# Turning the FFN input of blocks 1 to 5 to channels: 120 TensorE transposes, or VectorE 32x32 blocks and transfers between partitions

## The chip, the cores and the metric

The kernel runs on one NeuronCore of a Trainium2 chip. The metric is the device time of one execution in microseconds, as the median of several runs. Times inside an execution come from a profile of one execution.

## The reference, cut to what matters

One layer of an encoder, over 128 sample tokens (8 sequences of 16) and 2048 prompt tokens, width 1024, all float32:

```python
h = rmsnorm(x, g_pre_mix) * (1 + sc1) + sh1          # adaLN; sc, sh, gt from silu(c) @ w_ada
proj = h @ w_in                                       # 1024 -> 2176
ya, yb, yc = pool_mixer(proj), conformer_conv(proj), short_conv(proj)
x = x + gt1 * rmsnorm(concat(ya, yb, yc) @ w_out, g_post_mix)
h = rmsnorm(x, g_pre_ffn) * (1 + sc2) + sh2           # "FFN input" below
f = (silu(h @ w_gate) * (h @ w_up)) @ w_down          # 1024 -> 2816 -> 1024
x = x + gt2 * rmsnorm(f, g_post_ffn)
```

## The kernel before, in words

The 17 tiles of 128 tokens are worked in six blocks: block 0 has two tiles, blocks 1 to 5 three each (`NT`). Every weight is streamed from HBM for every block in units of 128 x 1024 floats (512 KB). A unit is split into a high and a low float32r part: ScalarE writes `whi` (`high`, L980), VectorE `wlo` (`low`, L1377), and TensorE does three float32r matmuls in place of one in float32. Units are named by what they are for: `in` (17 per block, ORDER), `out` (8), `gu` (gate and up, 44) and `dn` (down, 22). For a block c of 1 to 4 the order of units (STREAM) is: out of block c, in of block c+1, dn of block c-1, gu of block c. Block 5 has no `in` units after its `out`.

Nothing is scheduled at run time. Each engine has its own instruction list, written out by hand, and runs it strictly in order; semaphores tie the lists together. Three distances matter here:

- SyncE issues the transfer of unit n when TensorE is done with unit n-6 (`RING` = 6, `load`, L476), that is, as TensorE begins unit n-5.
- ScalarE and VectorE split unit n+4 at the place of unit n in their lists (`LEAD` = 4, `ahead`). At the place of `in` unit j ScalarE's list has `ahead("in", c+1, j)` first, so the split of the unit four further on, and behind it `evacuate(c+1, j)`, which copies the finished projection out of PSUM (L1068, L1075). At the place of `dn` unit k it has the split of unit k+4 and behind it `hidden_high(c-1, k+2)`, the high part of the hidden activations for `dn` unit k+2 (L1141); VectorE has the low part (L1429) in the same way.
- TensorE's `project(c+1, j)` waits until `evacuate(c+1, j-2)` has freed its PSUM bank, and `down(c-1, k)` for the high and low hidden activations of k.

The FFN input of block c is made this way. ScalarE normalises the three token tiles from `xr` into `xt` (L1013), token-major: 128 tokens on the partitions, 1024 channels along the free axis. TensorE needs channels on the partitions. So during the `dn` units of block c-1, after unit 6, 8, ... 20, TensorE turns one chunk of 128 channels of three tiles: three transposes (L720) against the identity into a PSUM bank. ScalarE adds scale and shift while it copies out (`modulate`, L1048, into `h_f`) and writes the high part (`h_split`, L1059); VectorE writes the low part (`h_rest`, L1422). 8 chunks x 3 tiles x 5 blocks are 120 transposes. Block 0 does the same at another place and isn't changed. The projection input of blocks 2 to 5 (`by_channel`) is loaded from HBM with channels first and has no transposes.

Of the kernel before, what the change touches and what calls it, by code (L numbers as in the profile page):

```python
# [17 lines left out]
TB = 3  # L18
# [160 lines left out]


def transposed(q):

    return sum(not by_channel(i) for i in range(q))

# [43 lines left out]
def build(nc, x_all, x_cols, c_all, consts, consts_a, cols, gpost, b_ada, w_ada, w_mix, w_pool, w_gu, w_dn,  # L228
# [3 lines left out]
    with ctx:  # L232
# [31 lines left out]
        xt = sb("xt", [P, TB, D])  # L264
        xr = sb("xr", [P, TB, D])
        junk = sb("junk", [P, D], BF16)
        ssq_x = sb("ssq_x", [P, TB])
# [70 lines left out]
        xn_ready = sem("xn_ready")  # L338
        t_full = sem("t_full")
        t_read = sem("t_read")  # L340
        sample_mod = sem("sample_mod")
# [74 lines left out]
        def sum_bank(r, t):  # L416

            return 0 if r == RES.index(("mix", NB - 1)) and t == 0 else 2 + 2 * t

        def bank_pair(bank):  # L420
            return ps[:, bank:bank + 2, :].rearrange("p a n -> p (a n)")
# [16 lines left out]
        def h_float(q, k):  # L438
            if NORMS[q][1] == 0:
                return (h_wait if q else h_first)[:, k, :]  # L440
            if by_channel(q):
                return x_chunk(k)
            return h_f[:, k % 2, :]
# [15 lines left out]
        def _(sp):  # L459
# [85 lines left out]
            load_four(7)  # L545

            def store_gate(i):
                sp.wait_ge(gates_made, i + 1)
                sp.dma_start(gates[i], (gate1, gate2)[i][0:ROWS, :]).then_inc(gates_stored, 16)
# [21 lines left out]
            for c in range(NB):  # L571
# [9 lines left out]
                if c + 1 < NB:  # L581
                    for j in range(0 if c else EARLY, NIN):
                        load("in", c + 1, j)
                        if c == 0 and j == EARLY:
                            load_gate(0)
                        if c == 0 and j == NIN - 3:
                            store_gate(1)
                        if c == 0 and j == NIN - 1:
                            load_gate(1)
                        if c == 0 and j == EARLY + 2:  # L590
                            store_states(False)
                        if j == 12:
                            store(x1_v, "mix", c)
                        if j == 15 and c:
                            wait_stored("mix", c)
                            sp.wait_ge(xn_ready, transposed(norm("F", c) + 1))
                            load_res(x1_v, c - 1)
                if c:
                    for k in range(NF):
                        load("dn", c - 1, k)  # L600
                        if c == NB - 1 and k == 11:
                            store(x1_v, "mix", c)
                        if c == NB - 1 and k == 14:
                            wait_stored("mix", c)
                            sp.wait_ge(xn_ready, transposed(norm("F", c) + 1))
                            load_res(x1_v, c - 1)
                for m in range(NF):
                    for i in range(2):
                        load("gu", c, m, i)
                    if m == 4 and c + 2 < NB:  # L610
                        sp.wait_ge(t_full, KD * transposed(norm("F", c) + 1))
                        if c:
                            sp.wait_ge(res_tiles, res_all(RES.index(("ffn", c - 1))))
                        sp.dma_start(xt[:, :, :].rearrange("p t d -> p (t d)"), x_cols[c]).then_inc(cols_landed, 16)
                    if m == 7 and c:
                        store(y_v, "ffn", c - 1)
                    if m == 9:
                        if c:
                            wait_stored("ffn", c - 1)
                        else:  # L620
                            wait_stored("mix", 0)
                            sp.wait_ge(xn_ready, transposed(norm("F", 0) + 1))
# [25 lines left out]
        def _(pe):  # L648
# [62 lines left out]
            def transposes(q, k):  # L711
                if k == 0:
                    pe.wait_ge(xn_ready, transposed(q + 1))
                if q == norm("F", 0) and k < 2:
# [116 lines left out]
            def gate_up(b, m):  # L831
                q, w = norm("F", b), NT[b] * P
                for i in range(2):
# [3 lines left out]
                    elif m == 0 and b == 0:  # L837
                        pe.wait_ge(evac_done, evac_count(1, NIN - 2))
                    elif m == 0:
                        pe.wait_ge(t_read, KD * q + KD - 1 + i)  # L840
                    elif i == 0:
# [94 lines left out]
            for c in range(NB):  # L936
# [37 lines left out]
        def _(act):  # L974
# [56 lines left out]
            def modulate(q, k):  # L1031
# [20 lines left out]
            def h_split(q, k):  # L1052
# [4 lines left out]
                if q == norm("F", 0):  # L1057
                    act.wait_ge(*((h_free, k + 1) if k < KD - 1 else (w_used, UNIT["in", 1, NIN - 1] + 1)))
                nc.scalar.activation(h_hi[:, k, 0:w], h_float(q, k)[:, 0:w], ACT.Copy).then_inc(h_hi_ready, 1)  # L1059

# [157 lines left out]
            for c in range(NB):  # L1218
# [29 lines left out]
                if c:  # L1248
                    if c + 1 == NB:
                        mix_squares("mix", c)  # L1250
                    for k in range(NF):
# [9 lines left out]
                        ch = (k - 6) // 2  # L1261
                        if k >= 6 and k % 2 == 0 and ch < KD:
                            modulate(norm("F", c), ch)
# [97 lines left out]
        def _(dve):  # L1361
# [49 lines left out]
            def scale(q, k):  # L1411
# [19 lines left out]
            def weigh(kind, b, i):  # L1431
# [3 lines left out]
                if i == 0:  # L1435
# [3 lines left out]
                    else:  # L1439
                        dve.wait_ge(t_full, KD * transposed(norm("F", c) + 1 if c < NB else len(NORMS)))  # L1440
                dve.wait_ge(mix_ssq, tiles_before_res(r) + i + 1)
# [314 lines left out]
            for c in range(NB):  # L1756
# [35 lines left out]
                if c:  # L1792
# [3 lines left out]
                    for k in range(NF):  # L1796
# [3 lines left out]
                        if c + 1 == NB and k < NT[c]:  # L1800
                            join("mix", c, k)
                        ch = (k - 6) // 2
                        if k >= 6 and k % 2 == 0 and ch < KD:
                            h_rest(norm("F", c), ch)
# [127 lines left out]
```

## Time and profile before

| | us |
|---|---|
| median of 3 runs (lowest, highest) | 2260.72 (2260.14, 2261.42) |
| span of the profiled execution, first to last instruction | 2256.9 |
| TensorE busy in it | 2241.4 |
| VectorE busy | 1348.1 |
| ScalarE busy | 1003.7 |
| GpSimd busy | 38.2 |
| share of the 16 DMA engines used by queue 1 | 47.8% |

The profiled execution is reported by its span, 2256.9 us; a whole execution has besides that what lies before the first and after the last instruction. The median of the runs is 3.8 us above the span. TensorE's granted clock is 0.999 of full speed. Durations of matmuls in the trace overlap: the hardware pipelines them, so the distance between two starts is the time that one takes of the engine. "SPq" rows are SyncE's issues of transfers: the time is that of the issuing, which holds back the next instruction of SyncE, not that of the transfer.

### The profile page before, as it was taken

What the parts mean: (1) busy time and instruction counts of PE and PEld (TensorE: products, weight loads), DVE (VectorE), ACT (ScalarE), POOL (GpSimd) and SP (SyncE); (2) the same over time, 40 slices, a digit from 0 to 9 for tenths busy, and PEclk for the clock granted to TensorE, in tenths of its full rate; (3) what the DMA queues carried; (4) which work ended last, traced back from release to release, by engine and by line L of the source; (5) the groups of instructions that cost most, each with busy time, mean ns of one, the idle gap of its engine ahead of it and who ended that gap; (6) DMA issues with size and microseconds to landing.
All of it is one profiled execution on the core that took longest, in us unless ns stands there. A gap on an engine that the chain in (4) does not pass through costs nothing.

```text
span 2256.9 us, 29984 instructions
## 1 busy us (share of the span) xinstructions
PE 2241.4 (99%) x12270; PEld 2069.5 (92%) x12270; DVE 1348.1 (60%) x1967; ACT 1003.7 (44%) x1419; POOL 38.2 (2%) x83
## 2 busy tenths in 40 slices
PE   9999999999999999999999999999999999999998
PEld 6779998979999988999898899989899998899987
DVE  3779966698444677744467854357784535443343
ACT  3455465454354534344544435254443425432332
POOL 0000000000000000000000000000000000000000
PEclk9999999999999999999999999999999999999999
DMA  9864654554443533544353363435335444444332
GB/s 375 310 218 168 239 202 140 177 169 166 170 151 129 181 127 122 186 150 154 126 185 123 123 213 122 157 123 187 122 127 181 123 131 154 154 150 159 123 129 94
DMA packets 103046, 368.98 MB, mean 163 GB/s; under 512 B 12631, under 2 KB 14807, under 8 KB 102396
## 3 DMA queue, kind: packets, MB, share of 16 engines
q1 hardware_dynamic: 102910, 367.06, 47.8%
q8 instruction: 98, 1.61, 0.3%
q14 instruction: 38, 0.31, 0.0%
HBM read 348.02 MB, written 19.00 MB: 163 GB/s over the span
## 4 chain that ended last, share of the span: by engine, by line
PE 89%; DVE 4%; DMA 1%; ACT 1%; issue 0%; SPq 0%; DVEq 0%; ACTq 0%
PE ps L650 89%; DVE wlo L1377 2%; DVE pr L1528 1%; DMA raw<-in_w_mix 1%; PE ps L720 1%; DVE early L1528 1%; PE ps L680 0%; DVE g_lo L1429 0%; ACT whi L980 0%; DVE h_lo L1422 0%; DMA raw<-in_w_gu 0%; ACT h_f L1048 0%; DVE xt L1446 0%; ACT junk L1003 0%; DVE pr L1550 0%
## 5 line engine op out<-in xcount | busy, mean ns | idle before, releaser
L1377 DVE TENSOR_TENSOR wlo<-raw,whi 128x1024 fp32r<-128x1024 f32 x531 | 646.6, 1222 | 521.9 <-ACT whi L980 520.6
L650 PE MATMUL ps<-h_hi,whi 128*128 128x384 f32 (+1 forms) x2808 | 920.9, 328 | 1.8 <-DVE h_lo L1422 1.0
L980 ACT ACTIVATE whi<-raw 128x1024 fp32r<-128x1024 f32 x531 | 560.8, 1058 | 811.6 <-DMA raw<-in_w_gu 528.7
L650 PE MATMUL ps<-h_hi,wlo 128*128 128x384 f32 (+1 forms) x2808 | 919.3, 327 | 0.0
L650 PE MATMUL ps<-h_lo,whi 128*128 128x384 f32 (+1 forms) x2808 | 919.2, 327 | 0.0
L650 PEld LDWEIGHTS ps<-h_hi,whi 128*128 128x128 f32 x2808 | 528.4, 188 | 7.0 <-issue 4.7
L650 PEld LDWEIGHTS ps<-h_lo,whi 128*128 128x128 f32 x2808 | 528.4, 188 | 0.5
L650 PEld LDWEIGHTS ps<-h_hi,wlo 128*128 128x128 f32 x2808 | 528.4, 188 | 0.0
L650 PE MATMUL ps<-whi,g_hi 128*128 128x512 f32 x748 | 235.1, 395 | 1.7 <-issue 0.9
L650 PE MATMUL ps<-whi,g_lo 128*128 128x512 f32 x748 | 231.1, 390 | 0.0
L650 PE MATMUL ps<-wlo,g_hi 128*128 128x512 f32 x748 | 230.8, 390 | 0.0
L1528 DVE SCALAR_TENSOR_TENSOR pr<-u,col,pr 128x384 f32<-128x384 f32 x360 | 208.3, 613 | 1.0
L1837 DVE TENSOR_TENSOR g_f<-ps,s_buf 128x384 f32<-128x384 f32 (+1 forms) x132 | 70.3, 533 | 218.3 <-PE ps L650 218.1
L650 PEld LDWEIGHTS ps<-wlo,g_hi 128*128 128x128 f32 x748 | 140.4, 188 | 29.9
L650 PEld LDWEIGHTS ps<-whi,g_lo 128*128 128x128 f32 x748 | 140.4, 188 | 29.7
L650 PEld LDWEIGHTS ps<-whi,g_hi 128*128 128x128 f32 x748 | 136.8, 188 | 31.1 <-DVE g_lo L1429 4.1
L650 PE MATMUL ps<-whi,y_pr 128*128 128x512 f32 x476 | 131.1, 389 | 0.0
L1068 ACT ACTIVATE pr<-ps 128x384 f32<-128x384 f32 (+1 forms) x84 | 39.3, 470 | 153.5 <-PE ps L650 153.4
L650 PEld LDWEIGHTS ps<-whi,y_pr 128*128 128x128 f32 x476 | 89.2, 188 | 18.3
L1048 ACT ACTIVATE h_f<-ps,shsc 128x384 f32<-128x384 f32 x48 | 32.2, 670 | 140.4 <-PE ps L720 125.5
L1422 DVE TENSOR_TENSOR h_lo<-h_f,h_hi 128x384 fp32r<-128x384 f32 x48 | 26.7, 557 | 83.7 <-ACT h_hi L1059 83.7
L1429 DVE TENSOR_TENSOR g_lo<-g_f,g_hi 128x384 fp32r<-128x384 f32 (+1 forms) x132 | 69.9, 529 | 11.4 <-ACT g_hi L1141 11.4
(148 smaller groups left out, 1313.6 us busy)
## 6 DMA issues: line engine op xcount, KB each, us to landing
raw<-in_w_gu SPq DMA_DIRECT2D x264, 512.0 KB, 3.3
raw<-in_w_mix SPq DMA_DIRECT2D x150, 512.0 KB, 3.3
raw<-in_w_dn SPq DMA_DIRECT2D x132, 512.0 KB, 3.3
xr<-in_x_all SPq DMA_DIRECT2D x29, 512.0 KB, 5.9
xr<-x_all SPq DMA_DIRECT2D x17, 512.0 KB, 5.8
pre<-in_w_ada SPq DMA_DIRECT2D x16, 512.0 KB, 10.4
x_all<-xr SPq DMA_DIRECT2D x5, 1536.0 KB, 7.5
xr<-in_w_ada SPq DMA_DIRECT2D x12, 512.0 KB, 7.9
```

Source lines behind the costliest of these rows:

```text
L650: return nc.tensor.matmul(out, lhsT, rhs, start=start, stop=stop, skip_group_check=True)
L720: last = nc.tensor.transpose(ps[:, t_bank(q, k), t * P:(t + 1) * P], xt[:, t, k * P:(k + 1) * P], ident)
L980: nc.scalar.activation(whi[:, s, :], raw[:, s, :], ACT.Copy).then_inc(w_hi, 1)
L1048: nc.scalar.activation(h_float(q, k)[:, c0:w], src, ACT.Identity, scale=shsc[:, 2 * ph + 1, k, 0:1], bias=shsc[:, 2 * ph, k, 0:1])\
L1068: i = nc.scalar.activation(dst, src, ACT.Sigmoid if kind == "g" else ACT.Copy)
L1377: tt(wlo[:, s, :], raw[:, s, :], whi[:, s, :].bitcast(F32), ALU.subtract).then_inc(w_lo, 1)
L1422: tt(h_lo[:, k, 0:w], h_float(q, k)[:, 0:w], h_hi[:, k, 0:w].bitcast(F32), ALU.subtract)\
L1429: tt(g_lo[:, s, 0:w], g_f[:, k, 0:w], g_hi[:, s, 0:w].bitcast(F32), ALU.subtract).then_inc(g_lo_ready, 1)
L1528: i = stt(z, conv_in(j, k), wk, src, ALU.mult, ALU.add)
L1837: tt(g_f[:, m, 0:w], ps[:, gu_bank(m, 1), 0:w], s_buf[:, m % 2, 0:w], ALU.mult).then_inc(g_ready, 1)
```

## The change

For blocks 1 to 5 (`turned`), the 120 transposes leave TensorE's list. VectorE turns each normalised token tile in 32x32 blocks, from `xt` into a new buffer `turn` (`turn_tile`, one instruction of 128 x 1024 floats a tile, 15 in all). That leaves every 32x32 block turned within its own strip of 32 partitions. SyncE then moves strip a's blocks to the strips where their channels belong (`turn_back`): for each tile 4 x 4 transfers, each of 32 partitions x 8 chunks x 32 floats, so 256 runs of 128 bytes and 32 KB; 48 transfers a block, 240 in all. They write into `xt`, now with channels on the partitions, and ScalarE's `modulate` works in place there and no longer reads PSUM or writes `h_f`. The waits that stood on the transposes move to other semaphores; in block 5 the eight chunks are made at `dn` units 13 to 20, one each, in place of every second one of 6 to 20. The scratch memory for GpSimd's transfers, of which there are none, is cut to 1024 bytes, which makes room for `turn`.

```diff
+def turned(q):
+    return NORMS[q][0] == "F" and NORMS[q][1] >= 1
+def f_chunks(c, k):
+    at = k - 13 if c == NB - 1 else (k - 6) // 2 if k % 2 == 0 else -1
+    return [at] if 0 <= at < KD else []
...
+            def turn_back(b):
+                q = norm("F", b)
+                sp.wait_ge(turn_full, turned_tiles(q + 1))
+                for t in range(NT[b]):
+                    for a in range(STRIPS):
+                        for s in range(STRIPS):
+                            src = strips(turn[:, t, :], a).rearrange("p (k m) -> p k m", k=KD)[:, :, C_PAD * s:C_PAD * (s + 1)]
+                            n0 = t * P + C_PAD * a
+                            dst = strips(xt[:, :, :].rearrange("p t d -> p (t d)").rearrange("p (k n) -> p k n", k=KD), s)
+                            sp.dma_start(dst[:, :, n0:n0 + C_PAD], src).then_inc(turn_landed, 16)
...
                             load_res(x1_v, c - 1)
+                        if j == 16 and c:
+                            turn_back(c)
...
                         if c == NB - 1 and k == 14:
                             wait_stored("mix", c)
...
                             load_res(x1_v, c - 1)
+                            turn_back(c)
...
                         down(c - 1, [k])
-                        ch = (k - 6) // 2
-                        if k >= 6 and k % 2 == 0 and ch < KD:
-                            if ch == 0 and c + 1 < NB:
-                                pe.wait_ge(evac_done, evac_count(c + 1, NIN - 1))
-                            transposes(norm("F", c), ch)
...
+                elif turned(q):
+                    act.wait_ge(turn_landed, 16 * STRIPS * STRIPS * turned_tiles(q + 1))
+                    src = x_chunk(k)[:, c0:w]
...
+            def turn_tile(b, t):
+                q = norm("F", b)
+                dve.wait_ge(xn_ready, normalised(q + 1))
+                if t == 0:
+                    dve.wait_ge(turn_landed, 16 * STRIPS * STRIPS * turned_tiles(q))
+                nc.vector.transpose(turn[:, t, :], xt[:, t, :]).then_inc(turn_full, 1)
...
+                        if c and j0 + 7 <= j < j0 + 7 + NT[c]:
+                            turn_tile(c, j - j0 - 7)
...
+                        if c + 1 == NB and k == 5:
+                            for t in range(NT[c]):
+                                turn_tile(c, t)
```

SyncE's list around the step from the `in` units of block 3 to the `dn` units of block 1, before (w_mix is `in` and `out`, the store and `xr` loads are residuals):

```order
L488 DMA x_all<-xr 128x3x1024
L476 DMA raw<-in_w_mix 128x1024 x3
L484 DMA xr<-x_all 128x1024 x3
L476 DMA raw<-in_w_mix 128x1024
L476 DMA raw<-in_w_dn 128x1024 x22
```

and the same place now:

```order
L515 DMA x_all<-xr 128x3x1024
L503 DMA raw<-in_w_mix 128x1024 x3
L511 DMA xr<-x_all 128x1024 x3
L503 DMA raw<-in_w_mix 128x1024
L583 DMA xt<-turn 32x8x32 x48
L503 DMA raw<-in_w_dn 128x1024 x22
```

The 48 transfers of the block stand between the last `in` unit's load and the first `dn` unit's.

ScalarE's list at the last `in` units of block 3, the same before and now but for line numbers (whi is the split of the unit four ahead; pr and xa are evacuations of the unit itself, here units 12 to 16; g_hi is hidden activations):

```order
L980 ACTIVATE whi<-raw 128x1024
L1068 ACTIVATE pr<-ps 128x384
L980 ACTIVATE whi<-raw 128x1024
L1068 ACTIVATE pr<-ps 128x384
L980 ACTIVATE whi<-raw 128x1024
L1068 ACTIVATE pr<-ps 128x384
L980 ACTIVATE whi<-raw 128x1024
L1075 ACTIVATE xa<-ps 128x384
L1141 ACTIVATE g_hi<-g_f 128x384
L980 ACTIVATE whi<-raw 128x1024
L1075 ACTIVATE xa<-ps 128x384
L1141 ACTIVATE g_hi<-g_f 128x384
```

The second whi here is that of `dn` unit 0, and the evacuation of `in` unit 13 stands behind it. Nothing moved.

VectorE's list at the `in` units 7 to 9 of block 3, now (u and pr are steps of the depthwise convolution):

```order
L1423 TENSOR_TENSOR wlo<-raw,whi 128x1024
L1470 STREAM_TRANSPOSE turn<-xt 128x1024
L1581 SCALAR_TENSOR_TENSOR pr<-u,col,pr 128x384 x3
L1423 TENSOR_TENSOR wlo<-raw,whi 128x1024
L1470 STREAM_TRANSPOSE turn<-xt 128x1024
L1555 TENSOR_TENSOR u<-pr 128x384
L1581 SCALAR_TENSOR_TENSOR pr<-u,col,pr 128x384
L1578 TENSOR_SCALAR pr<-u,col 128x384
L1423 TENSOR_TENSOR wlo<-raw,whi 128x1024
L1470 STREAM_TRANSPOSE turn<-xt 128x1024
```

Before, the same rows stood there without the three STREAM_TRANSPOSE.

## Rows read from the trace of the kernel before

**Rows 1.** The page: its head and part 1 (busy us, share, instructions).
```profile
span 2256.9 us, 29984 instructions
PE 2241.4 (99%) x12270; PEld 2069.5 (92%) x12270; DVE 1348.1 (60%) x1967; ACT 1003.7 (44%) x1419; POOL 38.2 (2%) x83
```
**Rows 2.** Waits, whole span: who waited for whom, us in total, times, longest.
```profile
ACT h_f L1048 <- PE ps L720: 125.5, 37, 4.5
PE ps L650 <- DVE g_lo L1429: 0.7, 4, 0.2
```
**Rows 3.** The chain of waits in block 2's dn units: start us, us, what.
```profile
837.77 8.21 PE ps L650 x36
846.30 8.21 PE ps L650 x36
```
**Rows 4.** Timeline of SyncE, block 2: start us, us, engine line op.
```profile
780.17 1.33 SPq L484 DMA_DIRECT2D xr<-x_all  x3
783.90 0.33 SPq L476 DMA_DIRECT2D raw<-in_w_mix  x1
788.06 21.13 SPq L476 DMA_DIRECT2D raw<-in_w_dn  x6
```
**Rows 5.** Timeline of ScalarE, block 2, places of in units 13 and 14.
```profile
792.61 1.05 ACT L980 ACTIVATE whi<-raw 128x1024 fp32r<-128x1024 f32 x1
796.39 0.49 ACT L1068 ACTIVATE pr<-ps 128x384 f32<-128x384 f32 x1 [2.72 <-PE ps L650]
...
800.55 0.49 ACT L1068 ACTIVATE pr<-ps 128x384 f32<-128x384 f32 x1 [2.72 <-PE ps L650]
```
**Rows 6.** The page, part 6: transfers, KB each, median us to landing.
```profile
raw<-in_w_dn SPq DMA_DIRECT2D x132, 512.0 KB, 3.3
```
**Rows 7.** Timeline of SyncE, issues of other shapes.
```profile
192.38 3.67 SPq L556 DMA_DIRECT2D gate_first<-gates  x8
...
1776.22 0.56 SPq L569 DMA_DIRECT2D out_o_pool_p<-xa  x1
1776.82 0.62 SPq L569 DMA_DIRECT2D out_o_conv_p<-u  x1
1777.48 0.63 SPq L569 DMA_DIRECT2D out_o_sconv_p<-su  x1
```
**Rows 8.** DMA, 1776 to 1780 us: packets, and issues with us to landing.
```profile
DMA packets 1216, 0.59 MB, mean 147 GB/s; under 512 B 1088, under 2 KB 1088, under 8 KB 1216
...
out_o_conv_p<-u SPq DMA_DIRECT2D x1, 45.0 KB, 5.7
out_o_pool_p<-xa SPq DMA_DIRECT2D x1, 15.0 KB, 3.5
out_o_sconv_p<-su SPq DMA_DIRECT2D x1, 3.0 KB, 7.2
```
**Rows 9.** DMA, 53 to 60 us, with four loads of 64 x 256 bytes.
```profile
DMA packets 802, 2.93 MB, mean 419 GB/s; under 512 B 87, under 2 KB 87, under 8 KB 801
...
w_pl<-in_w_pool SPq DMA_DIRECT2D x4, 16.0 KB, 12.2
```
**Rows 10.** Timeline of VectorE, block 2, place of in unit 9.
```profile
777.76 1.23 DVE L1377 TENSOR_TENSOR wlo<-raw,whi 128x1024 fp32r<-128x1024 f32 x1 [1.51 <-ACT whi L980]
```
**Rows 11.** Windows in dn units of blocks 1 and 2: busy us of PE, PEld, DVE, ACT, POOL.
```profile
457.00:516.00 59.00, 58.35 (x257) 45.67 (x256) 59.00 (x100) 33.87 (x53) 0.00 (x0) 1.00 0.54 178
...
810.00:870.00 60.00, 60.00 (x271) 49.58 (x271) 47.62 (x76) 26.52 (x38) 0.00 (x0) 1.00 0.40 130
```
**Rows 12.** Timeline of SyncE, block 5, dn units 14 and 15.
```profile
1920.94 1.34 SPq L484 DMA_DIRECT2D xr<-x_all  x3
1924.96 25.93 SPq L476 DMA_DIRECT2D raw<-in_w_dn  x7
```
**Rows 13.** Timeline of ScalarE, block 5, place of dn unit 11 and after unit 12.
```profile
1930.52 1.04 ACT L980 ACTIVATE whi<-raw 128x1024 fp32r<-128x1024 f32 x1
1931.47 0.51 ACT L1141 ACTIVATE g_hi<-g_f 128x384 fp32r<-128x384 f32 x1
...
1937.92 0.67 ACT L1048 ACTIVATE h_f<-ps,shsc 128x384 f32<-128x384 f32 x1 [3.83 <-PE ps L720]
```

More of the change, by code:

```diff
@@ L178, in loads_before_norm, with normalised, turned_tiles @@
     return sum(NT[b] for kind, b in NORMS[:q] if kind == "M" and b < 2)
+def turned(q):
+    return NORMS[q][0] == "F" and NORMS[q][1] >= 1
+def normalised(q):
+    return sum(not by_channel(i) for i in range(q))
 def transposed(q):
-    return sum(not by_channel(i) for i in range(q))
+    return sum(not by_channel(i) and not turned(i) for i in range(q))
+def f_chunks(c, k):
+    at = k - 13 if c == NB - 1 else (k - 6) // 2 if k % 2 == 0 else -1
+    return [at] if 0 <= at < KD else []
+def turned_tiles(q):
+    return sum(NT[NORMS[i][1]] for i in range(q) if turned(i))
 def tiles_before_res(r):
@@ L265, in build @@
         xr = sb("xr", [P, TB, D])
+        turn = sb("turn", [P, TB, D])
         junk = sb("junk", [P, D], BF16)
@@ L339, in build @@
         t_full = sem("t_full")
+        turn_full = sem("turn_full")
+        turn_landed = sem("turn_landed")
         t_read = sem("t_read")
@@ L418, in sum_bank, with strips @@
             return 0 if r == RES.index(("mix", NB - 1)) and t == 0 else 2 + 2 * t
+        def strips(ap, s):
+            return ap[C_PAD * s:C_PAD * (s + 1)]
         def bank_pair(bank):
@@ L440, in h_float @@
                 return (h_wait if q else h_first)[:, k, :]
-            if by_channel(q):
+            if by_channel(q) or turned(q):
                 return x_chunk(k)
@@ L595, in _ @@
                             wait_stored("mix", c)
-                            sp.wait_ge(xn_ready, transposed(norm("F", c) + 1))
+                            sp.wait_ge(xn_ready, normalised(norm("F", c) + 1))
                             load_res(x1_v, c - 1)
+                        if j == 16 and c:
+                            turn_back(c)
                 if c:
@@ L604, in _ @@
                             wait_stored("mix", c)
-                            sp.wait_ge(xn_ready, transposed(norm("F", c) + 1))
+                            sp.wait_ge(xn_ready, normalised(norm("F", c) + 1))
                             load_res(x1_v, c - 1)
+                            turn_back(c)
                 for m in range(NF):
@@ L610, in _ @@
                     if m == 4 and c + 2 < NB:
-                        sp.wait_ge(t_full, KD * transposed(norm("F", c) + 1))
+                        if turned(norm("F", c)):
+                            sp.wait_ge(h_lo_ready, KD * (norm("F", c) + 1))
+                        else:
+                            sp.wait_ge(t_full, KD * transposed(norm("F", c) + 1))
                         if c:
@@ L621, in _ @@
                             wait_stored("mix", 0)
-                            sp.wait_ge(xn_ready, transposed(norm("F", 0) + 1))
+                            sp.wait_ge(xn_ready, normalised(norm("F", 0) + 1))
                         if c + 2 < NB:
@@ L712, in transposes @@
                 if k == 0:
-                    pe.wait_ge(xn_ready, transposed(q + 1))
+                    pe.wait_ge(xn_ready, normalised(q + 1))
                 if q == norm("F", 0) and k < 2:
@@ L838, in gate_up @@
                         pe.wait_ge(evac_done, evac_count(1, NIN - 2))
+                    elif m == 0 and b + 1 < NB:
+                        pe.wait_ge(evac_done, evac_count(b + 1, NIN - 2 + i))
                     elif m == 0:
-                        pe.wait_ge(t_read, KD * q + KD - 1 + i)
+                        pe.wait_ge(mix_read, res_tile(RES.index(("mix", b)), 0))
                     elif i == 0:
@@ L1058, in h_split @@
                     act.wait_ge(*((h_free, k + 1) if k < KD - 1 else (w_used, UNIT["in", 1, NIN - 1] + 1)))
+                if turned(q):
+                    b = NORMS[q][1]
+                    act.wait_ge(w_used, UNIT[("in", b + 1, NIN - 1) if b + 1 < NB else ("gu", b - 1, NF - 1, 1)] + 1)
                 nc.scalar.activation(h_hi[:, k, 0:w], h_float(q, k)[:, 0:w], ACT.Copy).then_inc(h_hi_ready, 1)
@@ L1260, in _ @@
                                 x_normalise(norm("F", c), t)
-                        ch = (k - 6) // 2
-                        if k >= 6 and k % 2 == 0 and ch < KD:
+                        for ch in f_chunks(c, k):
                             modulate(norm("F", c), ch)
@@ L1439, in weigh @@
                     else:
-                        dve.wait_ge(t_full, KD * transposed(norm("F", c) + 1 if c < NB else len(NORMS)))
+                        dve.wait_ge(h_lo_ready, KD * (norm("F", c) + 1 if c < NB else len(NORMS)))
                 dve.wait_ge(mix_ssq, tiles_before_res(r) + i + 1)
@@ L1801, in _ @@
                             join("mix", c, k)
-                        ch = (k - 6) // 2
-                        if k >= 6 and k % 2 == 0 and ch < KD:
+                        if c + 1 == NB and k == 5:
+                            for t in range(NT[c]):
+                                turn_tile(c, t)
+                        for ch in f_chunks(c, k):
                             h_rest(norm("F", c), ch)
@@ L1914 @@
                 o_conv_s=(P, NCONV, SEQS, HIST + STEPS), o_sconv_s=(P, NSC, SEQS, SHIST + STEPS))
-    nc = bacc.Bacc("TRN2", target_bir_lowering=False, num_devices=1)
+    nc = bacc.Bacc("TRN2", target_bir_lowering=False, num_devices=1, dynamic_dma_scratch_size=1024)
     ins = {k: c(v) for k, v in ins.items()}
```

## The prediction, made before the changed kernel was run

> **What bounds the kernel now.** I read the head of the page first: TensorE is busy 2241.4 of 2256.9 us [rows 1]. The list of waits then shows that hardly anything holds it up: its entry for VectorE's g_lo is 0.7 us in all, while ScalarE waits 125.5 us for the transposes and loses nothing by it [rows 2]. So everything that leaves TensorE's list is gained, and everything that makes TensorE wait is paid in full. The rest of the question is which of the other lists are close to making it wait. The timelines of SyncE and ScalarE [rows 4, 5] are the place to look, because the change puts 240 transfers into the one list that feeds the weights.
>
> **What leaves TensorE.** In the chain of waits two stretches of 36 matmuls (two dn units, 8.21 us) begin 8.53 us apart [rows 3]; the 0.32 us between is what the three transposes of one chunk cost. Eight chunks are 2.6 us a block. In block 1 this is not gained: its dn units work on the two tiles of block 0, are short, and VectorE is the bound there, busy 59.00 of 59.00 us while the weight loads of TensorE fill only 45.67; in block 2 it is busy 47.62 of 60.00 [rows 11]. So four blocks gain: 4 x 2.6 = 10.4 us.
>
> **What VectorE and ScalarE get.** Three 32x32 turns of 128x1024 floats a block. The trace has no such instruction. The nearest row is the split of the same size, 1.23 us, with 1.51 us of idle before it [rows 10]; three turns are 3.7 us, spread over three in units of 4.16 us each, where VectorE has about that idle, and it catches up behind them. I cost them at nothing. The cover is the wait of SyncE: the last turn is needed at 784.3 us [rows 4], and it starts behind a split that begins at 777.76 [rows 10]. So even a turn of 4 us in place of 1.2 would just be in time; beyond that each us counts once a block. The lower bound is nothing as well, since no work of VectorE goes. ScalarE's scale and shift reads SBUF in place of PSUM with the same number of instructions, and its 125.5 us of waits go; it is not the bound, so again nothing.
>
> **What SyncE gets, and what is queued behind it.** I follow block 2. The load of in unit 16 is issued at 783.90 and takes 0.33; that of dn unit 0 followed at 788.06 [rows 4]. Now 48 transfers stand between. Let p be the time from one issue to the next.
>
> Rows for p: 128 runs of 4 KB, 1.33/3 = 0.44 us [rows 4]; only 16 runs, 3.67/8 = 0.46 [rows 7]; the stores of pool (256 runs of 60 bytes) and conv (384 runs of 120 bytes) start 0.60 and 0.66 before the next [rows 7]; a single weight load is issued in 0.33 [rows 4]. So the issue has a fixed part and grows a little with the number of runs. A transfer of the change has 256 runs of 128 bytes. I take p = 0.60, the row with as many runs, and keep 0.33 and 0.66 as ends of what the issue costs.
>
> 48 x 0.60 = 28.8 us. The load of dn unit 0 is issued at 784.3 + 28.8 = 813.1 and lands 3.3 us later [rows 6], at 816.4. An in unit lasts 4.16 us (783.90 to 788.06 is one). TensorE needs dn unit 0 itself only at about 809, two units after 800.55, but something else is needed earlier. In ScalarE's list the split of dn unit 0 (792.61) stands ahead of the evacuation of in unit 13 (796.39) [rows 5], and TensorE waits for that evacuation before in unit 15, which starts at 800.55, when the next evacuation does [rows 5]. So ScalarE stands at the split until 816.4, takes 1.05, evacuates in 0.49, and in unit 15 starts at 817.9 in place of 800.5: TensorE stands still for 17.4 us. In general this wait is 48p - 11.4 us. Behind it the other loads need no more waiting for free buffers: they are issued 0.4 us apart, split at 1.1 us each, and TensorE needs one every 4.1 us, so the wait is paid once.
>
> It comes once in each of blocks 1 to 4, since the order of the lists is the same. In block 5 the 48 transfers stand behind the residual loads at 1920.94, which end at 1922.3, and in front of dn unit 15, issued at 1924.96 before [rows 12]. ScalarE's split of that unit (1930.52) stands ahead of the hidden activations for dn unit 13 (1931.47) [rows 13]. Now: 1922.3 + 28.8 + 3.3 + 1.04 + 0.51, and the same for VectorE's low part (of the same size), about 1956.5. Dn unit 13 would start at 1936.9: the 1937.92 of [rows 13] less three chunks of transposes. The wait is 19.6 us, or 48p - 9.2. The data of the transfers themselves are asked for only by ScalarE's scale and shift at dn unit 6 (13 in block 5), behind these waits, and hold up nothing more.
>
> **The sum.** Block 1: +17.4. Blocks 2, 3 and 4: 3 x (17.4 - 2.6) = +44.4. Block 5: +19.6 - 2.6 = +17.0. Together +78.8 us on the profiled execution, whose span is 2256.9; the median of the runs is 3.8 us above it, and I add the change to the median: 2260.7 + 78.8 = 2339.5, forecast 2340. As a formula the change is 240p - 65.2: with p = 0.33 it is +14 (2275), with 0.44 +40 (2301), with 0.46 +45 (2306), with 0.66 +93 (2354).
>
> By the page "DMA: Bandwidth & Descriptors" of the Trainium skill, section "Issuing engines are not separate DMA queues", the time that a sequencer needs to initiate a DMA is usually small beside the DMA itself. Taken alone this says that 48 issues cost little, and it is the rival "hidden" below. The trace half agrees, 0.33 to 0.66 us of issue against 3.3 to landing; but it is 48 issues in one list that count here, not one.
>
> **The rivals.**
>
> Rival A, the DMA engines are the bound and not the issue. Each of the 16 engines gets 48 x 16 = 768 runs a block in the same queue as the weights. For it: the three small stores, issued 0.60 and 0.66 apart, land after 3.5, 5.7 and 7.2 us [rows 8], so 2.8 and 2.2 us apart; the 384 runs of the second are 24 for an engine, 0.117 us a run. At that, 768 runs take 90 us a block, 61 more than the issue: 5 x 61 = +305, 2645 us. Against it: these stores go to HBM. Four loads of 64 runs of 256 bytes into SBUF stand in a stretch that still moves 419 GB/s and land no later than that crowded stretch explains [rows 9]. Half way, at 0.05 us a run, it is 38.4 us a block, 2388. The point from which it decides is 0.60/16 = 0.0375 us a run.
>
> By the same page, section "Why small descriptors are slow (HBM only)", transfers within SBUF don't suffer from small pieces. By that rule rival A has little chance, and no row here shows a transfer from SBUF to SBUF; I leave it a chance for that reason.
>
> Rival B, hidden and faster. If the lead of the loads covers the burst, only the gain is left: 2260.7 - 10.4 = 2250. The wait is gone where 48p is under 11.4, p under 0.24; with p under 0.27 the gain still outweighs it. For it: SyncE waits for TensorE nearly all the time and has time on average. Against it: every issue in the rows takes at least 0.33 us, and the lead is 16.6 us, of which landing, split and evacuation take 4.8.
>
> Rival C, the turns are the bound: VectorE's 32x32 turn at more than 4 us each, SyncE waiting for it. Each us beyond that is paid in each block: at 6 us, 5 x 3 x 2 = +30 on top of the forecast, 2370. Nothing in the trace speaks for it.
>
> That the transposes don't leave TensorE is excluded: its list has 40 rows fewer, each of three transposes.
>
> **How the numbers follow.** Forecast (issue-bound, p from 0.39 to 0.70, 2289 to 2363) 0.75; rival A 0.13; rival B 0.05; rival C 0.02; issue-bound with p under 0.39, 0.05. The predicted time is 2340. The range 2290 to 2400 leaves out rival B, the cheap issue, and the part of A above 0.05 us a run. A measurement of this kernel tells 0.2%, 4.5 us, from no change. Faster than that needs rival B: 0.05. Within it needs p between 0.25 and 0.29: 0.02. Slower: 0.93.
>
> **What would show it.** In the changed profile the chain of waits should have, in each of blocks 1 to 5, one stretch of SyncE issues of about 29 us for x48, then one landing of a dn unit, one whi and one evacuation (in block 5 one g_hi, g_lo), and in the list of waits TensorE should stand five times for 17 to 20 us. The time from one issue of a turn transfer to the next gives p. The transfers should land some 2 to 4 us after their issue; if they land later and later within the burst, rival A is right. VectorE's turns should take about 1.2 us and end before 784. TensorE's dn units of block 2 should come without the 0.32 us gaps. It is wrong if TensorE's waits come at the scale and shift, at the end of the turns, or not at all.

## The result, and the profile after

| | before | after |
|---|---|---|
| median of the runs, us (lowest, highest) | 2260.4 (2259.3, 2261.4) | 2369.8 (2367.6, 2372.2) |
| ratio to before, 95% interval | 1 | 1.0488 (1.0475 to 1.0500) |
| span of the profiled execution, us | 2256.9 | 2366.2 |
| TensorE busy, us | 2241.4 | 2239.3 |
| mean granted clock of TensorE | 0.999 | 0.974 |

The changed kernel is 109.4 us slower, where 78.8 was forecast. The head of its page, against [rows 1] (TensorE 12270 instructions there, 12150 here):

```profile
span 2366.2 us, 30005 instructions
PE 2239.3 (95%) x12150; PEld 2067.5 (87%) x12150; DVE 1365.4 (58%) x1982; ACT 1006.1 (43%) x1419; POOL 37.0 (2%) x83
```

TensorE's list of waits (engine and line, whom it waited for, us in total, times, longest), against [rows 2]:

```profile
PE ps L694 <- ACT pr L1115: 83.2, 4, 21.0
PE ps L694 <- DVE g_lo L1482: 28.8, 8, 25.6
```

Four waits of 20.8 us for an evacuation and one of 25.6 us for the low hidden activations: the five places named ahead. The other seven waits for g_lo, 3.2 us together, are in the dn units of block 1 (0.7 before): there VectorE is the bound, and the transposes' time isn't gained, as forecast. SyncE's timeline at block 2, against [rows 4]:

```profile
807.65 0.33 SPq L503 DMA_DIRECT2D raw<-in_w_mix  x1
808.02 31.70 SPq L583 DMA_DIRECT2D xt<-turn  x48
839.77 28.43 SPq L503 DMA_DIRECT2D raw<-in_w_dn  x9
```

Before, the first dn load was issued 4.16 us after the last in load, now 32.1 us. The 48 issues take 31.7 us, so p = 0.66 where 0.60 was forecast. What follows them is in the chain of waits (start us, us, what), and after it ScalarE's evacuation in its timeline, against [rows 5]:

```profile
839.77 3.60 DMA raw<-in_w_dn
843.39 1.06 ACT whi L1021
844.88 364.72 PE ps L694 x1922
```

```profile
843.39 1.06 ACT L1021 ACTIVATE whi<-raw 128x1024 fp32r<-128x1024 f32 x1 [26.93 <-DMA raw<-in_w_dn]
844.36 0.47 ACT L1115 ACTIVATE pr<-ps 128x384 f32<-128x384 f32 x1
```

ScalarE stands 26.93 us at the split of dn unit 0, the evacuation of in unit 13 comes right behind it, and TensorE starts at 844.88. TensorE's own timeline there has something that the prediction did not have:

```profile
844.88 0.69 PE L694 MATMUL ps<-h_hi,whi 128*128 128x384 f32 x1 [20.62 <-ACT pr L1115]
845.37 0.52 PE L694 MATMUL ps<-h_lo,whi 128*128 128x384 f32 x1
845.69 0.52 PE L694 MATMUL ps<-h_hi,wlo 128*128 128x384 f32 x1
...
849.21 0.45 PE L694 MATMUL ps<-h_lo,whi 128*128 128x384 f32 x1
849.50 0.34 PE L694 MATMUL ps<-h_hi,wlo 128*128 128x384 f32 x1
849.67 0.34 PE L694 MATMUL ps<-h_hi,whi 128*128 128x384 f32 x1
```

The starts are 0.32 us apart and from 849.50 on 0.17. The granted clock says why (window, us, PE busy and count, clock, DMA share, GB/s):

```profile
844.00:849.00 5.00, 4.12 (x13) 0.50 0.60 228
849.50:900.00 50.50, 50.50 (x232) 1.00 0.36 125
```

Behind the wait TensorE runs at 0.50 of its clock, 1.2 in place of 2.4 GHz, for 14 matmuls. They take 4.62 us where 14 x 0.1733 = 2.43 would do, so 2.2 us are lost. Behind the five waits 10 to 17 matmuls are that slow, for 4.3 to 5.5 us; counted in the same way, 11.4 us are lost in all.

The transfers and the turns (part 6 of the page; then the rows of both instructions: ns min/median/max):

```profile
xt<-turn SPq DMA_DIRECT2D x240, 32.0 KB, 2.0
```

```profile
L583 SPq DMA_DIRECT2D xt<-turn x240: 585/611/1514, 429.0 to 2039.8; - x120
L1470 DVE STREAM_TRANSPOSE turn<-xt x15: 1202/1237/1239, 416.5 to 1993.4; 128x1024 f32<-128x1024 f32 x15
```

### The profile page after: what moved, and what is told of

It is laid out like the page before. It is cut to its first block, busy times and chain, and to the rows that moved or that the text cites. A ratio compares the mean times of both kernels' runs of the same rounds, so it can differ in the third digit from the quotient of the medians.

```text
span 2366.2 us, 30005 instructions
## 1 busy us (share of the span) xinstructions
PE 2239.3 (95%) x12150; PEld 2067.5 (87%) x12150; DVE 1365.4 (58%) x1982; ACT 1006.1 (43%) x1419; POOL 37.0 (2%) x83
## 4 chain that ended last, share of the span: by engine, by line
PE 83%; SPq 6%; DVE 4%; DMA 1%; issue 1%; ACT 1%; DVEq 0%; ACTq 0%
PE ps L694 82%; SPq L583 6%; DVE wlo L1423 1%; DVE pr L1581 1%; DMA raw<-in_w_dn 1%; DMA raw<-in_w_gu 0%; PE ps L724 0%; ACT whi L1021 0%; DVE g_lo L1482 0%; DVE early L1581 0%; DVE h_lo L1475 0%; ACT junk L1044 0%; ACT h_f L1092 0%; PE ps L764 0%; DVE pr L1603 0%
## 5 line engine op out<-in xcount | busy, mean ns | idle before, releaser
L694 PE MATMUL ps<-h_hi,whi 128*128 128x384 f32 (+1 forms) x2808 | 925.7, 330 | 84.7 <-ACT pr L1115 83.2
L694 PE MATMUL ps<-whi,g_hi 128*128 128x512 f32 x748 | 233.1, 393 | 29.7 <-DVE g_lo L1482 28.8
L1188 ACT ACTIVATE g_hi<-g_f 128x384 fp32r<-128x384 f32 (+1 forms) x132 | 65.5, 496 | 9.4 <-PE ps L694 9.3
L1322 ACT ACTIVATE s_buf<-ps 128x384 f32<-128x384 f32 (+1 forms) x132 | 61.2, 464 | 5.4 <-PE ps L694 4.9
```

What stands on the lines that cost most here:

```text
L694: return nc.tensor.matmul(out, lhsT, rhs, start=start, stop=stop, skip_group_check=True)
L1188: nc.scalar.activation(g_hi[:, at % G_RING, 0:w], g_f[:, k, 0:w], ACT.Copy).then_inc(g_hi_ready, 1)
L1322: nc.scalar.activation(s_buf[:, m % 2, 0:w], ps[:, gu_bank(m, 0), 0:w], ACT.Silu)\
```

## The experiments

Times are medians, ratios are to the kernel before on the same chip.

| | transfers a block | us | ratio (95%) | issue burst, us | wait, blocks 1 to 4, us each | block 5, us |
|---|---|---|---|---|---|---|
| after | 48 | 2369.8 | 1.0488 (1.0475 to 1.0500) | 31.9 | 20.8 | 25.6 |
| e1_third | 16 | 2258.2 | 0.9984 (0.9974 to 0.9994) | 10.9 | 0.5 | 3.1 |
| e3_half | 24 | 2292.2 | 1.0138 (1.0122 to 1.0154) | 16.6 | 6.0 | 8.3 |
| e2_small | 48, 4 KB | 2363.1 | 1.0448 (1.0432 to 1.0465) | 31.0 | 20.3 | 22.5 |
| e8_long | 48, runs of 1 KB | 2363.4 | 1.0452 (1.0433 to 1.0471) | 31.1 | 20.4 | 23.1 |
| e9_wide | 48, 128 partitions | 2367.1 | 1.0474 (1.0433 to 1.0515) | 31.5 | 20.5 | 24.0 |
| e10_hbm | 48, from HBM | 2324.3 | 1.0285 (1.0248 to 1.0321) | 23.2 | 12.5 | 14.8 |
| e4_swap | 48 | 2364.9 | 1.0454 (1.0436 to 1.0473) | 32.2 | 18.7 | 25.7 |
| e5_merged | 16, 96 KB | 2285.8 | 1.0113 (1.0098 to 1.0129) | 15.1 | 4.6 | 8.2 |
| e6_spread | 48, spread | 2252.5 | 0.9962 (0.9949 to 0.9974) | 12 x 2.6 to 3.8 | none | 1.3 |
| e7_merged_spread | 16, spread | 2249.9 | 0.9952 (0.9939 to 0.9964) | 8 x 1.3 to 2.9 | none | 0.8 |

The burst is the mean of blocks 1 to 4, the wait of these blocks TensorE's total for ScalarE's evacuation over four, that of block 5 the longest for g_lo.

### Does the number of issues set the wait?

e1_third and e3_half leave transfers out, so their output is not the reference's. The counts that ScalarE and VectorE wait for shrink with them; VectorE's turns stay:

```diff
-                for t in range(NT[b]):
-                    for a in range(STRIPS):
+                for t in range(2):                                        # e1_third: range(1)
+                    for a in range(STRIPS if t == 0 else STRIPS // 2):    # e1_third: STRIPS
```

> Only the 16 transfers of the first of the three tiles are made (the FFN input of the other two tiles is left untransposed, so the output isn't the reference's). Theory S (SyncE's issues stand in front of the weight loads and are paid by their number above a lead of 11.4 us): 16 x 0.66 = 10.6 us is under the lead, no wait of TensorE over 2 us, and only the gain of the missing transposes is left: 2260.4 - 10.4 = 2250. TensorE's clock stays at its upper level. Rival F (a wait that comes once a block whatever the number: for the turns, or the first landing): about 2370 as with 48. Rival H (the transposes were in truth hidden and their going gains nothing): 2260.

> 24 of the 48 transfers a block (half of the FFN input is left untransposed). Theory S: 24 x 0.66 = 15.9 us, a wait of 4.5 us in blocks 1 to 4 and about 7.5 in block 5, 25.5 in all; less 10.4: 2275.5 if TensorE's clock doesn't fall after such a short wait, up to 2286 if it falls as after the long ones. Rival F: 2370.

The wait follows the burst less 11.4 us: 16.6 - 11.4 = 5.2 (measured 6.0), 31.9 - 11.4 = 20.5 (20.8), and for 10.9 next to nothing. Rival F, a wait that comes once whatever the number, falls. e3_half took 2292, above the 2275 to 2286 that I expected. The clock fell after waits as short as 5.25 us, which the upper figure allows for; the rest is in the waits, 23.8 + 8.3 = 32.1 us where 25.5 were expected.

e1_third gains 3.6 us and not 10. The period from one block's last in load to the next one's is 379.2 us (789.92 to 1169.14), 381.98 before (783.90 to 1165.88): the 2.8 us of the transposes are there. Three things take 6.9 of the 10.4 us back: the wait of 3.1 us in block 5, 1.7 us at half the clock behind it, and 2.1 us in three waits for the evacuation. For e1_third the lead is just about used up.

### What does one issue cost?

e2_small moves one chunk in place of eight; e8_long 32 runs of 1 KB; e9_wide the same bytes over 128 partitions; e10_hbm reads as many bytes in the same shape as e8_long from HBM. All four leave wrong values. Each line below goes on with `.then_inc(turn_landed, 16)`, cut here:

```diff
-sp.dma_start(dst[:, :, n0:n0 + C_PAD], src)
+sp.dma_start(dst[:, 0:1, n0:n0 + C_PAD], src[:, 0:1, :])                                                 # e2_small
+sp.dma_start(strips(xt[:, t, 256 * a:256 * a + 256], s), strips(turn[:, t, 256 * s:256 * s + 256], a))   # e8_long
+sp.dma_start(xt[:, t, 256 * a + 64 * s:256 * a + 64 * s + 64], turn[:, t, 256 * a + 64 * s:256 * a + 64 * s + 64])   # e9_wide
+sp.dma_start(strips(xt[:, t, 256 * a:256 * a + 256], s), strips(x_v[:, T0[b] + t, 256 * s:256 * s + 256], a))        # e10_hbm
```

> All 48 transfers a block, but each moves one chunk of 32 partitions x 32 floats in place of eight: 32 runs and 4 KB in place of 256 and 32 KB (most of the FFN input is left out). Theory S with an issue price that is mainly fixed: p falls from 0.66 to about 0.46 (the row with 16 runs), waits 4 x 10.7 + 12.9 = 55.7 us, less 10.4 for the transposes, plus about 10 for the clock: 2316. If the price goes with the runs, p about 0.33 and 2280. If it is the same for every three-dimensional pattern, p 0.66 and 2370. Rival A (the data of 128-byte runs): an eighth of it, so no wait beyond the issue.

> 48 transfers a block in the changed kernel's place, with the same 32 KB each, but as 32 runs of 1 KB between strips of 32 partitions (the FFN input is then not channels-first: wrong values, same work). It tells what sets the 0.66 us of one issue. If it is the short run of 128 bytes: p falls to the 0.44 of a weight load, waits 4 x 9.7 + 11.9, about 2310. If it is that both sides lie in SBUF or that only 32 partitions are named: p stays 0.65 and the time is that of e2_small, 2363.

> 48 transfers a block in the changed kernel's place, 32 KB each, from turn to xt, but over all 128 partitions, 64 floats each (no exchange between strips: wrong values). e8_long left open what makes one issue 0.65 us. If it is that only 32 partitions are named: p falls to 0.44 here, the waits are 4 x 9.7 + 11.9 = 50.7, and the time is about 2261 - 10.4 + 50.7 + 10 for the clock = 2311. If it is that both sides lie in SBUF: p 0.65, 2363.

> 48 transfers a block of 32 partitions x 256 floats, as in e8_long, but read from x_all in HBM and not from SBUF (wrong values). If it is both sides in SBUF that make the issue 0.65 us: p about 0.45, 2311 to 2316. If it is the 32 partitions: p 0.65, 2363. It tests the formula of the wait (48p - 11.4 in blocks 1 to 4, 48p - 9.2 in block 5) at another p in either case.

SyncE's burst of block 2 in e2_small, e9_wide and e10_hbm:

```profile
808.37 31.26 SPq L583 DMA_DIRECT2D xt<-turn  x48
```

```profile
813.03 31.70 SPq L583 DMA_DIRECT2D xt<-turn  x48
```

```profile
803.98 23.02 SPq L583 DMA_DIRECT2D xt<-in_x_all  x48
```

An eighth of the data, longer runs and four times the partitions leave p at 0.65. Reading from HBM brings it to 0.48. So the length and number of the runs, from which I had argued by the stores in [rows 7], don't set p, nor does the shape; taking the source from HBM makes it cheaper. Whether it is the source in SBUF alone or both sides in SBUF stays open, since no run changes the destination. The stores from SBUF to HBM speak both ways: the small ones of [rows 7] take 0.56 to 0.63 us each, the residual store 0.44 (SyncE's timeline of the changed kernel):

```profile
791.38 0.44 SPq L515 DMA_DIRECT2D x_all<-xr  x1
```

e10_hbm tests the formula at another p: 23.2 - 11.4 = 11.8, measured 12.5.

### Is it the row that the wait was said to come through?

e4_swap exchanges two rows of ScalarE's list:

```diff
+                        late = c and j == NIN - RING + 2
+                        if not late:
-                        ahead("in", c + 1, j)
+                            ahead("in", c + 1, j)
...
                         evacuate(c + 1, j)
+                        if late:
+                            ahead("in", c + 1, j)
```

> All transfers, in the changed kernel's place, but ScalarE evacuates in unit 13 before it splits dn unit 0 (the only two rows exchanged). If the wait reaches TensorE through the evacuation that stands behind that split, the next thing behind it is the evacuation of in unit 14, needed one unit (4.16 us) later: four waits shorter by 4.2 us, 2369.8 - 16.6 = 2353, block 5 unchanged. Rival (TensorE waits for dn unit 0's weights themselves): the same time as the changed kernel, 2370.

The waits became shorter, by 2.1 us each and not 4.2, and the time is 2365 and not 2353. ScalarE's timeline shows the rest:

```profile
821.49 0.49 ACT L1115 ACTIVATE pr<-ps 128x384 f32<-128x384 f32 x1 [3.67 <-PE ps L694]
845.02 1.06 ACT L1021 ACTIVATE whi<-raw 128x1024 fp32r<-128x1024 f32 x1 [23.04 <-DMA raw<-in_w_dn]
846.62 1.06 ACT L1021 ACTIVATE whi<-raw 128x1024 fp32r<-128x1024 f32 x1 [0.54 <-DMA raw<-in_w_dn]
847.58 0.47 ACT L1115 ACTIVATE pr<-ps 128x384 f32<-128x384 f32 x1
```

The evacuation of in unit 13 is now in time (821.49), but that of unit 14 stands behind two splits, of dn unit 0 and of dn unit 1, and the second costs 1.6 us: 0.54 of waiting for its data and 1.06 of work. My figure left that one out. The time moved, so the rival (TensorE waits for the weights of dn unit 0 themselves) falls, and the path is as predicted.

### Are the DMA engines far from being the bound?

e5_merged moves all three tiles in one transfer; VectorE writes `turn` so that chunk and tile are one axis:

```diff
-nc.vector.transpose(turn[:, t, :], xt[:, t, :])
+nc.vector.transpose(turn[:, t:KD * TB:TB, :], xt[:, t, :].rearrange("p (k m) -> p k m", k=KD))
...
+                for a in range(STRIPS):
+                    for s in range(STRIPS):
+                        src = strips(turn, a)[:, :, C_PAD * s:C_PAD * (s + 1)]
+                        dst = strips(xt[:, :, :].rearrange("p t d -> p (t d)").rearrange("p (g m) -> p g m", g=KD * TB), s)
+                        yield dst[:, :, C_PAD * a:C_PAD * (a + 1)], src
```

> The same data in 16 transfers a block in place of 48: VectorE writes the turned tiles so that chunk and tile form one axis, and one transfer moves 32 partitions x 24 x 32 floats (768 runs of 128 bytes). Same place in SyncE's list. Theory S with a price per issue and not per run (e2_small: 0.65 with 32 runs, after: 0.66 with 256): 16 x 0.7 = 11.2 us, no wait in blocks 1 to 4, about 2 to 3 us in block 5, as e1_third: 2258. Rival (the price goes with the runs after all, 768 in place of 256: p about 0.9 to 1.5): waits of 3 to 13 us a block, 2275 to 2325. Rival A (the 16 DMA engines are the bound: 768 runs each at once, in a third of the time): the first weight load behind the burst lands later than 3.2 us.

The burst takes 15.7 us in block 2 where 16 x 0.7 = 11.2 were expected, and the time is 2286 and not 2258. SyncE's timeline; then queue 1 from 791 to 812 us (packets, MB, and the time that the packets took as a share of 16 engines' time), and last the same for the changed kernel's burst, 808 to 845 us:

```profile
791.15 15.72 SPq L585 DMA_DIRECT2D xt<-turn  x16
```

```profile
q1 hardware_dynamic: 13225, 4.07, 99.2%
```

```profile
q1 hardware_dynamic: 13798, 4.29, 50.5%
```

Here the DMA engines hold SyncE up. e7_merged_spread issues the same 16 transfers in pairs, most of them at 1.28 us a pair, 0.64 each; here they take 0.98 each. The weight and residual loads at both ends of the window are part of the 99.2%. From 802 to 806 us only the turned data moved:

```profile
q1 hardware_dynamic: 4267, 0.54, 92.7%
```

0.54 MB in 4 us is 134 GB/s, or 0.015 us for a run on one of the 16 engines; over the whole burst, 768 runs in 15.7 us, it is 0.020. So rival A names something real, but in the changed kernel a transfer needs at most 16 x 0.020 = 0.33 us of the engines and 0.66 of SyncE. Its transfers don't land later and later either. In block 2 the first seven took 3.0 to 5.5 us, while loads issued before them still kept the queue 90.1% busy (808 to 812 us), and the later ones 2.0.

### Does anything remain when the issues aren't in the way?

In blocks 1 to 4 e6_spread takes the same 48 transfers in fours behind twelve weight loads, and e7_merged_spread e5_merged's 16 in pairs behind eight. In block 5 they are six behind each of eight loads and four behind each of four, and e6_spread makes the scale and shift there at dn units 17 to 20, two chunks each:

```diff
                         if j == 16 and c:
-                            turn_back(c)
+                            parts = turn_parts(c)
+                            take(parts, 4)                      # e7_merged_spread: 2
...
+                        if k <= 10 and c < NB - 1:              # k < 7
+                            take(parts, 4)                      # 2
+                        if c == NB - 1 and 13 <= k <= 20:       # 13 <= k < 17
+                            take(parts, 6)                      # 4
```

> The 48 transfers a block as in the changed kernel, but four behind each weight load from in unit 16 to dn unit 10 (block 5: six behind each of dn units 13 to 20, and its scale and shift at units 17 to 20, two chunks each). 4 x 0.66 + 0.33 = 3.0 us of issue in units of 4.16 and 4.08 us (2.72 in block 1), so no weight load is late by more than about 3 us. Theory S: no wait of TensorE over 1 us, clock at the upper level throughout: 2261 - 10.4 = 2251. Rival (the number of transfers costs something of its own, in the DMA engines or by the weights' landing): some way between 2251 and 2370 although no issue is in the way.

> Both: 16 transfers a block, two behind each weight load from in unit 16 to dn unit 6 (block 5: four behind each of dn units 13 to 16, scale and shift at 13 to 20 as in the changed kernel). Theory S: 2 x 0.7 + 0.33 = 1.7 us of issue a unit, every weight load on time: 2251, faster than the kernel before by 0.4%. If issues that are on time cost the same whatever their number, e6_spread and this one take the same time within 3 us. Rival (the gain of the transposes is lost elsewhere, as VectorE's 3.7 us of turns a block): 2258 or more, as e1_third.

SyncE's timeline at block 2 in e6_spread:

```profile
786.91 0.33 SPq L505 DMA_DIRECT2D raw<-in_w_mix  x1
787.29 2.56 SPq L585 DMA_DIRECT2D xt<-turn  x4
791.08 0.34 SPq L505 DMA_DIRECT2D raw<-in_w_dn  x1
791.46 2.55 SPq L585 DMA_DIRECT2D xt<-turn  x4
```

The dn load goes out 4.17 us after the in load, on time. Both versions beat the kernel before, by 0.4 and 0.5%. The change costs 109 us with its 48 transfers in one place and gains 8 with them spread. Their number has next to no price of its own: 48 and 16 differ by 2.6 us, within the intervals, and 2.0 of them are waits for g_lo (6.5 us in all against 4.5). Of the 10.4 us of the transposes e7_merged_spread brings all, 11.0; VectorE's turns cost nothing that shows. Issuing the transfers from ScalarE's or GpSimd's queue was not tried.

### Can the clock's share be had back?

e11_busy and e12_busy_short give TensorE matmuls without use during the waits:

```diff
+            def busy(c, bank, count):
+                pe.wait_ge(mix_read, res_all(RES.index(("mix", c))))
+                for _ in range(count):
+                    mm(ps[:, bank, 0:P], ident, ident, True, True)
...
+                        if c and j == NIN - 2:
+                            busy(c, 7, 180)      # e12_busy_short: 85
...
+                        if c == NB - 1 and k == 13:
+                            busy(c, 1, 225)      # 105
```

> The changed kernel, and in each of its five waits TensorE multiplies the identity by itself into an unused PSUM bank (180 matmuls of 128 columns before in unit 15 in blocks 1 to 4, 225 before dn unit 13 in block 5; at 0.107 us each 19.3 and 24.1 us, shorter than the waits of 20.8 and 25.6). Nothing is computed with them. If each long wait costs some 2 us behind its end because TensorE's clock has fallen by then (14 matmuls at 0.32 in place of 0.173 us), these 10 us come back: 2370 - 10 = 2360, the granted clock near 1.0. If the matmuls behind the wait are slow for another reason, or the clock falls anyway: 2370.

> As e11_busy, whose matmuls took 0.224 us each and not 0.107, so that they outlasted the waits by some 20 us; now 85 and 105 of them, 19.0 and 23.5 us, shorter than the waits. If the clock's fall costs 2 us behind each wait: 2370 - 10 = 2360 with a granted clock near 1.0. If not: 2370.

e11_busy took 2458.6 us (1.0876, 1.0858 to 1.0894): a float32 matmul of 128 columns is 0.224 us and not the 0.107 of a transpose, so they lasted 40 us in place of 19. TensorE never waited there and its clock stayed at 0.998. That prices the fall of the clock from the other side. TensorE's timeline at block 2 (the matmul before these lines ends at 841.91):

```profile
841.75 40.36 PE L694 MATMUL ps<-con 128*128 128x128 f32 x360
...
881.86 0.42 PE L694 MATMUL ps<-h_hi,whi 128*128 128x384 f32 x1
```

From 841.91 to 881.86 are 39.95 us. It is as long in the other three blocks and 50.0 us in block 5, together 209.8 where the changed kernel waits 83.2 + 25.6 = 108.8. But the span is only 90.7 us longer (2456.9 against 2366.2) and not 101.0: 10.3 us come back where TensorE doesn't pause, near the 11.4 counted from the pace.

e12_busy_short took 2375.0 (1.0513, 1.0495 to 1.0530), no better than the changed kernel. Its timeline (the last of the idle matmuls ended at 845.96):

```profile
844.79 1.17 PE L694 MATMUL ps<-con 128*128 128x128 f32 x9
849.23 0.69 PE L694 MATMUL ps<-h_hi,whi 128*128 128x384 f32 x1 [3.27 <-ACT pr L1124]
849.72 0.52 PE L694 MATMUL ps<-h_lo,whi 128*128 128x384 f32 x1
...
854.52 0.48 PE L694 MATMUL ps<-h_lo,whi 128*128 128x384 f32 x1
854.83 0.34 PE L694 MATMUL ps<-h_hi,wlo 128*128 128x384 f32 x1
```

A pause of 3.27 us was left, and after it 17 matmuls ran at half the clock. The other four blocks kept pauses of 2.4 to 4.3 us, each with a slow stretch behind it. The burst had also become longer, 32.4 to 33.3 us in blocks 1 to 4; why is open. So the expectation of 2360 failed. That the matmuls behind a wait are slow by the clock is shown by the granted clock, by their pace and by the 10 us of e11_busy. With the burst left in its place, no version was found that gets these us back and is faster for it.

## Why the prediction was right, point by point

- **TensorE is the bound, and its waits are paid in full.** Right. The span of the profiled execution grew by 109.3 us. Its parts: 83.2 + 25.6 of waits, 11.4 of lowered clock, less 10.4 for the transposes: 109.8.
- **The transposes are worth 2.6 us a block.** Right: 2.8 in the period of e1_third, and 11.0 in all by e7_merged_spread.
- **The turns cost nothing.** Right: 1.24 us each (1.23 taken), and e7_merged_spread has them all. Rival C has nothing for it.
- **p = 0.60.** Mis-sized: 0.66, in block 5 0.70. With bursts of 31.9 and 33.7 us in place of 28.8 that is 17 us. The reason was wrong too: p doesn't go by the number of runs, so the pool store with as many runs gave nearly the right figure by chance. What makes an issue dear has to do with the source in SBUF, and the trace of before had no transfer within SBUF. In block 5 the first nine issues fell into a stretch with the queue 95.7% busy (2006 to 2014 us), and the slowest of them took 1.51 us.
- **48p - 11.4 us in blocks 1 to 4.** Right, for three lengths of the burst: with the measured ones it gives 20.5, 11.8 and 5.2 us, measured 20.8, 12.5 and 6.0. The place, the evacuation behind the split, was right. What is on top is the landing of dn unit 0, for which I had taken 3.3 us. In block 2 it is 3.60 us in the changed kernel and, in the chains of e10_hbm, e3_half and e5_merged,

```profile
827.05 3.96 DMA raw<-in_w_dn
```

```profile
811.52 3.82 DMA raw<-in_w_dn
```

```profile
806.92 4.30 DMA raw<-in_w_dn
```

  so 0.7, 0.5 and 1.0 us more than assumed. The waits there are 12.3, 5.25 and 5.3 us, where the bursts of that block less 11.4 give 11.6, 4.7 and 4.3.
- **48p - 9.2 us in block 5.** With the measured 33.7 us it gives 24.5, measured 25.6. Most of the missing us is a row of VectorE (0.7) and the landing (0.2): the chain there is (start us, us, what)

```profile
2040.48 3.48 DMA raw<-in_w_dn
2043.96 0.02 issue
2043.98 1.06 ACT whi L1021
2045.07 1.23 DVE wlo L1423
2046.30 0.48 DVE g_lo L1482
```

  I had put ScalarE's g_hi (0.51) between the split and g_lo. VectorE's wlo (1.23) stands there, and g_hi runs beside it.
- **A term that was missing: TensorE's clock.** 2.0 to 2.6 us behind each wait, 11.4 us in all. Nothing in [rows 1 to 13] had a pause from which to price it.
- **Rivals.** A: not the bound at p = 0.66 (from 824 to 836 us, in the middle of block 2's burst, the packets took 33.5% of the engines' time), though it is in e5_merged. B, hidden and faster: not as written, but it is what e6_spread and e7_merged_spread make come true. One transfer of the change takes 0.66 us of issue against 2.0 to landing, and 48 of them stand in the list that feeds the weights. The Trainium skill says on the page "DMA: Bandwidth & Descriptors", section "Issuing engines are not separate DMA queues", that the time to initiate a transfer is usually small beside the transfer. That is said of one transfer; here it is a third even for one.
- **The range.** The measured 2369.8 us lies in the stated 2290 to 2400, but above the 2289 to 2363 of the issue-bound case, which had the chance of 0.75. With the measured p the formula 240p - 65.2 gives 2354; the clock and the landings make the rest. The range reached past 2363 only for rival A, which is not what happened, so its upper part held by luck.

Two terms, p and the clock, make most of the 30.6 us between forecast and result: 17 and 11.4. The landings and the row of VectorE are the rest.

## What to carry to other kernels

A transfer costs its issuing engine time, here 0.3 to 0.7 us, and in an in-order list this is paid by whatever stands behind it: multiply the number of issues by their price and compare with the lead of the next load, counted to the first thing that its late landing holds up in any list, not to its own use. Here the transfers were all but free in the gaps between loads and cost 109 us in one burst. When a wait is put in front of TensorE, add to its length the slow stretch of its clock behind it, here 2.0 to 2.6 us a wait.

## What the runs showed of the hardware

- Issue on SyncE: 0.65 us from SBUF to SBUF, for 32 to 768 runs, 4 to 96 KB and 32 or 128 partitions; 0.48 from HBM to SBUF for 32 runs of 1 KB. When the DMA engines are full it is longer, 0.98 us in e5_merged.
- 128-byte runs within SBUF: 0.015 us each on a DMA engine when the 16 are nearly full (92.7%), 134 GB/s; [rows 9] has a stretch of 419 GB/s, most of it in packets of 4 KB. The short runs are dearer with the engines far from full too. These are queue 1 from 824 to 836 us in the changed kernel (128-byte runs) and in e8_long (1 KB):

```profile
q1 hardware_dynamic: 5043, 0.61, 33.5%
```

```profile
q1 hardware_dynamic: 904, 0.62, 21.0%
```

  For the same bytes the packets of the short runs take 1.6 times as long. The page "DMA: Bandwidth & Descriptors" of the Trainium skill says in "Why small descriptors are slow (HBM only)" that transfers within SBUF don't suffer from small pieces; the measurement disagrees.
- TensorE ran at half its clock (1.2 GHz) for 9 to 19 matmuls, 3.0 to 6.2 us, after pauses of 2.4 to 25.6 us (after, e2_small, e3_half, e10_hbm, e12_busy_short). The stretch doesn't grow with the pause: 17 matmuls behind 3.27 us and behind 20.98. In e5_merged a pause of 3.50 us in block 1 had none behind it.
- By [rows 3] a transpose of 128 columns takes 0.107 us of TensorE; a float32 matmul of the same size took 0.224 (40.36 us for 180).
